# Expert weights asked for in the order in which pairs free their slots, and unread products moved, in a two-layer decoder step

## What is computed

```python
def _hier_moe(x, w_coarse, b_coarse, w_fine, b_fine, w_gate_up, w_down):
    ...
    for g in range(N_GROUPS):
        gate_g = jnp.where((grp == g)[:, None], gates, 0.0).astype(x.dtype)
        hg, hu = jnp.split(jnp.einsum('nd,edf->nef', xt, w_gate_up[g]), 2, axis=-1)
        out = out + jnp.einsum('nef,efd->nd', jax.nn.silu(hg) * hu * gate_g[..., None], w_down[g])
```

## Time and profile before

| what | value |
|---|---|
| runs | 1246.79, 1242.51 and 1245.45 us; median 1245.45 |
| profiled execution | 1240.65 us, span 1238.7 us, 15277 instructions |
| TensorE | busy 1115.0 us (90% of the span), mean granted clock 0.955 |
| VectorE, ScalarE, GpSimd | 504.6, 225.7 and 180.6 us |
| HBM | 342.75 MB read, 31.16 MB written; 302 GB/s over the span |
| asks for expert weights | 96 + 32 for gate and up, 56 + 8 for down, 1024 KB each |

### The profile page before, as it was taken

One profiled execution on the slowest core, in us unless ns is written; L12 is line 12 of the kernel. 1 busy time (PEld: TensorE's weight loads), 2 busy tenths in 40 slices (PEclk: granted clock), 3 DMA queues, 4 the chain that ended last, 5 costly groups with the idle time before them and its releaser, 6 DMA issues. The chain is left out here.

```text
span 1238.7 us, 15277 instructions
## 1 busy us (share of the span) xinstructions
PE 1115.0 (90%) x5797; PEld 565.1 (46%) x5797; DVE 504.6 (41%) x1368; ACT 225.7 (18%) x507; POOL 180.6 (15%) x177
## 2 busy tenths in 40 slices
PE   8999999999999978877899899999899999887872
PEld 6874666655543323323444346544554433332230
DVE  3614666567642211112432314553888322111117
ACT  1311233311121100001411213243212111000000
POOL 0000000000011111100634643220000111110203
PEclk9999899999999999889999999989899999998895
DMA  7520110439479999997967988884976899999955
GB/s 286 198 90 1 73 69 1 145 125 421 179 249 420 420 421 420 421 420 292 394 241 256 400 331 351 320 319 158 357 325 238 304 415 418 420 421 421 423 209 216
DMA packets 84955, 358.84 MB, mean 290 GB/s; under 512 B 13943, under 2 KB 18172, under 8 KB 55180
## 3 DMA queue, kind: packets, MB, share of 16 engines
q1 hardware_dynamic: 63276, 279.57, 56.8%
q0 software_dynamic: 19520, 74.01, 15.5%
q10 hardware_dynamic: 2080, 4.19, 0.9%
HBM read 342.75 MB, written 31.16 MB: 302 GB/s over the span
## 5 line engine op out<-in xcount | busy, mean ns | idle before, releaser
L1854 PE MATMUL ahead_psum<-m_wg,top_xT 128*64 128x512 f32 x704 | 202.1, 635 | 35.0 <-DMA m_wg<-in_moe_w_gate_up 28.2
L1854 PEld LDWEIGHTS ahead_psum<-m_wg,top_xT 128*64 128x64 f32 x704 | 61.2, 146 | 147.5 <-issue 102.7
L1879 PE MATMUL n_psum_m<-m_wd,top_xT 128*64 128x512 f32 x456 | 121.8, 604 | 1.6 <-ACT top_xT L1938 1.0
L1854 PE MATMUL ahead_psum<-top_wide,top_xT 128*64 128x512 f32 x288 | 100.0, 625 | 12.5 <-DMA top_wide<-in_moe_w_gate_up 6.4
L1333 PE MATMUL ahead_psum<-top_wide,top_xT 128*128 128x512 f32 x224 | 102.6, 603 | 1.5 <-PEq L159 1.5
L1920 DVE COPY top_xT<-n_psum_t 128x512 f32<-128x512 f32 x31 | 21.4, 691 | 185.3 <-PE n_psum_t L1839 185.3
L2307 PE MATMUL ahead_psum<-top_wide,top_xT 128*128 128x512 f32 x192 | 85.3, 595 | 4.3 <-DVE top_xT L2913 4.3
L1771 POOL DMA_INDIRECT expert_rows<-e_Y,m_dest x33 | 32.8, 994 | 380.2 <-DVE e_Y L1929 339.5
L2111 POOL DMA_INDIRECT cd_kv<-in_cache_kT,top_kpages x64 | 62.0, 969 | 65.4 <-PE cd_psum_d L2350 43.8
L1879 PEld LDWEIGHTS n_psum_m<-m_wd,top_xT 128*64 128x64 f32 x456 | 35.5, 138 | 56.5 <-issue 53.7
L1333 PEld LDWEIGHTS ahead_psum<-top_wide,top_xT 128*128 128x128 f32 x224 | 41.0, 192 | 44.2 <-issue 44.0
(11 more groups left out here) (517 smaller groups left out, 1706.3 us busy)
## 6 DMA issues: line engine op xcount, KB each, us to landing
m_wg<-in_moe_w_gate_up SPq DMA_DIRECT2D x96, 1024.0 KB, 26.7
m_wd<-in_moe_w_down SPq DMA_DIRECT2D x56, 1024.0 KB, 27.3
top_wide<-in_moe_w_gate_up SPq DMA_DIRECT2D x32, 1024.0 KB, 24.2
cd_kv<-in_cache_kT SPq DMA_DIRECT2D x64, 256.0 KB, 5.6
top_X<-in_moe_w_down SPq DMA_DIRECT2D x8, 1024.0 KB, 23.0
ab_w<-in_ab_w_in SPq DMA_DIRECT2D x2, 2048.0 KB, 11.5
top_wide<-in_ab_w_in SPq DMA_DIRECT2D x2, 2048.0 KB, 7.8
top_wide<-in_ab_w_out SPq DMA_DIRECT2D x2, 2048.0 KB, 8.6
```

Of the source, the lines that this page charges most:

```text
L1854: last = nc.tensor.matmul(pg[i % 2][64 * a:64 * a + 64, :], xgT[i % 2][:, j, 64 * a:64 * a + 64], wg[E.slot(i, a)][:, j * 512:(j + 1) * 51 ...
L1879: last = nc.tensor.matmul(py[n2][64 * a:64 * a + 64, :], hT[:, j, 64 * a:64 * a + 64], wd[E.slot(i, a)][:, j * D + n2 * 512:j * D + (n2 + ...
```

## The change

The loads are the same, and each waits for the same semaphore counts as before. What changes is the order: for each pair p, SyncE waits for gh and asks for the h0 of both experts whose slots p frees, then waits for gu and asks for both h1, then for dn and asks for both down weights. Ahead of the end it asks for the up halves of experts 29, 30 and 31 before the down weights of 29, 30 and 31. The 12 unread products behind the last regular pair are dropped in both layers, and the attention stage opens with 12 calls instead of 6.

```diff
--- before.py
+++ after.py
@@ -1177,9 +1177,9 @@
             return (2 * i + a) % self.RING
         return (((4, 0), (1, 2)), ((5, 6), (4, 0)))[self.l][(i - NE // 2) % 2][a]
 
-    def left(self, n):
-
-        return (n - self.RING) // 2 + 1
+    def after(self, p):
+
+        return [n for n in (2 * p + self.RING, 2 * p + self.RING + 1) if n < NE]
 
     def load_up(self, eng, n, halves=(0, 1)):
         for h in halves:
@@ -1192,17 +1192,18 @@
         row = (self.l * NE + n) * 128
         eng.dma_start(self.wd[n % self.RING][:, :], self.w_dn[row:row + 128, :]).then_inc(self.down_in[n // 2 % 4], 16)
 
-    def reload_up(self, eng, n, half_used, multiplied):
-
-        eng.wait_ge(half_used, self.left(n))
-        self.load_up(eng, n, (0,))
-        eng.wait_ge(multiplied, self.left(n))
-        self.load_up(eng, n, (1,))
-
-    def reload_down(self, eng, n, projected):
-
-        eng.wait_ge(projected, self.left(n))
-        self.load_down(eng, n)
+    def reload_up(self, eng, p, half_used, multiplied):
+
+        for h, used in enumerate((half_used, multiplied)):
+            eng.wait_ge(used, p + 1)
+            for n in self.after(p):
+                self.load_up(eng, n, (h,))
+
+    def reload_down(self, eng, p, projected):
+
+        eng.wait_ge(projected, p + 1)
+        for n in self.after(p):
+            self.load_down(eng, n)
 
     def fill(self, eng):
         for i in range(2):
@@ -1806,17 +1807,14 @@
         pool.sem_inc(all_landed, 1)
 
     def sync(sp):
-        E.reload_up(sp, 7, gh, gu)
-        E.reload_down(sp, 7, dn)
-        for n in range(8, NE - 4, 2):
-            E.reload_up(sp, n, gh, gu)
-            E.reload_up(sp, n + 1, gh, gu)
-            E.reload_down(sp, n, dn)
-            E.reload_down(sp, n + 1, dn)
-        for n in range(NE - 4, NE):
-            E.reload_up(sp, n, gh, gu)
-        for n in range(NE - 4, NE):
-            E.reload_down(sp, n, dn)
+        last = (NE - 1 - E.RING) // 2
+        for p in range(last - 1):
+            E.reload_up(sp, p, gh, gu)
+            E.reload_down(sp, p, dn)
+        E.reload_up(sp, last - 1, gh, gu)
+        E.reload_up(sp, last, gh, gu)
+        E.reload_down(sp, last - 1, dn)
+        E.reload_down(sp, last, dn)
         if lines:
             sp.dma_start(X[0:1, 4, :], lines[0].partition_broadcast(1)).then_inc(line_in, 16)
             sp.dma_start(xT[0:1, 4:8, 256:512], lines[1].rearrange("(o k n) -> o k n", o=1, k=4)).then_inc(line_in, 16)
@@ -1906,7 +1904,6 @@
         x_T(2)
         gate_up(1, 1)
         run(2, main)
-        idle_products(nc, C, unread, 12)
         tiles = tiles_of(pe)
         for (lo, hi), least in zip(parts, (0, 2)):
             with pe.If(tiles > least):
@@ -2472,7 +2469,7 @@
                     p_values(i - 2)
 
             front, back = range(KD // 2), range(KD // 2, KD)
-            idle_products(nc, C, bc, 6)
+            idle_products(nc, C, bc, 12)
             normal(0)
             idle_products(nc, C, bc, 4)
             project("q", "part")
```

## The result

The changed kernel takes **1229.38 us** (median of four executions, 1227.55 to 1231.06) beside 1244.62 us (four, 1242.51 to 1246.79) for the kernel before: ratio 0.9878, 95% interval 0.9838 to 0.9918. That is 15.2 us faster. I had forecast 1234.9 us, range 1230 to 1242: the direction is right, and the time lies 0.6 us under the range. The profiled execution after took 1231.06 us (span 1229.2), 9.6 us less than that of before (1240.65, span 1238.7); the sum of my steps was 10.6 us.

What follows compares the result with a forecast made beforehand. Weight loads, not products, were taken to set the pace of the expert stages. The terms -2.4 - 0.8 - 3.0 - 4.4 sum to -10.6 us, taken from 1245.45 us: 1234.9 us, range 1230 to 1242.

Steps and rivals of the forecast that it cites:

- the last one of the sum: Whole kernel: the profiled execution's 4.8 us under the median of three runs is carried over, so 1245.45 - 10.6 us.
- Order and lead: Expert stages: new order of asks with two blocks' lead starts the last gate 2.4 us earlier in layer 0, 3.0 in layer 1.
- the hole: Start of the expert reloads: DMA engines partly idle, 6.4 us unused in layer 0, 7.0 us in layer 1.
- The products dropped: Behind the last regular pair: nothing gained in layer 0; layer 1 behind the gate 4.4 us faster, bounds -5.3 and -0.6.
- the register read: Layer 1's extra pair: reading the tile count, perhaps covered by the dropped products, becomes exposed, +0.9 us.
- the weights: Layer 1, gate_up(16, 0): its second weights land at 1181.5, in time by 1.7 us for a start at 1183.2.
- The head: Attention stage's start: twelve calls hide an instruction fetch, transposes come 0.8 us earlier; ends -0.8 and +2.7, at worst +5.3.
- The rival (the stall stays where it is, +2.7): Attention stage's head: stall tied to entering the stage, head costs +2.7 instead of -0.8, 1238.4 us; chance 0.25.
- The warm gate: gate_up(14, 0), both layers: short TensorE idleness gives 3.55 us at full clock, 4.5 us more gained, 1230.3 us; chance 0.06.
- The dry stream: Expert stages: queue runs short of asks, each pair loses 2.6 us, 39 us in all, some 1279 us; chance 0.03.
- the order without the lead: Expert stages: other traffic takes the idle DMA time, gate 2.5 us later per layer, 1245.3 us, no change; chance 0.08.

Runs made afterwards that it cites:

- null: The kernel before, run once more unchanged: median 1245.88 us (12 executions), ratio 0.9982 to the kernel before.
- after_again: The changed kernel run again unchanged, beside other executions of the kernel before: 1234.25 us, ratio 0.9913.
- after_third: The changed kernel run once more unchanged, beside other executions of the kernel before: 1232.57 us (12 executions), ratio 0.9942.
- unread13: The kernel before with 13 unread products behind the last pair in place of 12: 1248.77 us, one execution.
- order_only: The kernel before with only the new order of asks, 12 unread products and 6 head calls kept: 1238.28 us (12 executions), ratio 0.9936.
- before_late_gather: The kernel before, with GpSimd gathering the extra pair's weights only once the last down blocks have landed: 1248.18 us (12 executions), ratio 1.0019.
- before_fill: The kernel before plus two calls of unread products in both layers' settle stage, ahead of the last row tile's second transposes: 1243.48 us (12 executions), ratio 0.9988.
- no_lead: The changed kernel, but expert 8's halves wait behind expert 7's down weights as before; new order from pair 1: 1243.75 us (12 executions), ratio 0.9982.
- tail_order: The changed kernel with another order of the last 15 asks, the four down blocks last: 1237.28 us (11 executions), ratio 0.9908.
- drop_only: The kernel before with only the 12 unread products behind the last pair dropped: 1241.46 us (12 executions), ratio 0.9957.
- drop_order_head6: The changed kernel with 6 calls of unread products at the attention stage's head in place of 12: 1234.17 us (12 executions), ratio 0.9942.
- head_only: The kernel before with only the attention stage's head calls raised from 6 to 12: 1247.63 us (12 executions), ratio 1.0029.

## Why the prediction missed, step by step

**The step that failed is the last one of the sum**: "The profiled execution took 1240.65 us ..., which is 4.8 us under the median of the three runs; I carry the difference over". That treats the distance of one execution to a median as a constant of the kernel. It isn't. The profiled execution of the changed kernel lay 1.7 us *over* its median, and those of null, after_again and after_third lie 1.7, 1.8 and 0.7 us over theirs. The miss is made up so: profiled difference 9.6 us where the sum had 10.6, +1.0; distance to the median 4.8 + 1.7, -6.5; together -5.5, which is 1229.4 less 1234.9. The range failed with it. Its low end was a mechanism (a warm clock at the gate) and left nothing for the executions themselves, though 1240.65 to 1246.79 stood in front of me.

Luck has a part on both sides. The medians of the changed kernel over 11 and 12 executions, 1234.25 and 1232.57 us, lie 0.7 and 2.3 us from the forecast and inside its range: the miss is as much that of a median of four as of the forecast. And that the two profiled executions differ by nearly what I summed is no proof of the steps. Followed through the two traces, the difference is 0.3 us ahead of layer 0's first gate, 3.5 in its experts, 1.4 to the transposes of the attention stage, then 3.4 us *lost* up to layer 1's first gate, 3.2 gained in its experts and 4.5 behind them. The part in between is not the change's: from those transposes to that gate single traces take 363.5 to 371.9 us, and on the mean 367.4 us with the old order and 367.5 us with the new (nine and seven traces). The trace of before had one of the shortest, 363.9 us.

**What makes executions differ** is in the traces, mostly far from the change: how long TensorE's clock stays at its lower level. Layer 0's mixer, TensorE's timeline of null, of before and of unread13 (16 matmuls of line 511, and in unread13 a second fall some 12 us later, seen in line 568's eight passes):

```profile
135.17 7.13 PE L511 MATMUL ab_psum<-top_wide,top_xT 128*128 128x512 f32 x16
```

```profile
136.20 9.71 PE L511 MATMUL ab_psum<-top_wide,top_xT 128*128 128x512 f32 x16
...
151.81 1.06 PE L568 MATMUL ab_psum<-top_consts,ab_later 128*128 128x128 f32 x8
```

```profile
136.20 10.07 PE L511 MATMUL ab_psum<-top_wide,top_xT 128*128 128x512 f32 x16
...
155.10 1.92 PE L568 MATMUL ab_psum<-top_consts,ab_later 128*128 128x128 f32 x8
```

The granted clock there (the column ahead of the DMA share), null, before, then unread13 with both of its falls:

```profile
135.00:140.00 5.00, 5.00 (x18) 2.20 (x13) 2.25 (x4) 0.00 (x0) 0.00 (x0) 1.00 0.38 157
```

```profile
135.00:140.00 5.00, 5.00 (x17) 2.60 (x16) 2.52 (x5) 0.00 (x0) 0.00 (x0) 0.50 0.34 143
```

```profile
135.00:140.00 5.00, 5.00 (x21) 2.60 (x18) 2.87 (x5) 0.00 (x0) 0.00 (x0) 0.53 0.28 116
...
150.00:155.00 5.00, 5.00 (x23) 4.26 (x20) 3.24 (x8) 0.42 (x1) 0.00 (x0) 0.50 0.56 210
```

The code and the data are the same up to here. The first pair's gate of layer 0 starts at 343.60, 346.68 and 352.50 us. Over all 18 traces its start follows the clock: where TensorE ran at the lower level for 3.4 us up to it (1.7 us lost) it comes at 343.4 to 344.4 us, where for 20.5 us (10.2 us lost) at 352.3 to 352.6 us. The same is seen in the settle stage of layer 1, in two executions of the changed kernel (its own trace, then that of after_again), 20 passes that pick rows:

```profile
939.93 5.54 PE L1391 MATMUL ahead_psum<-top_X,m_xg 32*128 32x512 f32 x8
...
945.96 5.42 PE L1391 MATMUL ahead_psum<-top_X,m_xg 128*128 128x512 f32 x12
```

```profile
940.06 7.49 PE L1391 MATMUL ahead_psum<-top_X,m_xg 32*128 32x512 f32 x8
...
948.38 7.44 PE L1391 MATMUL ahead_psum<-top_X,m_xg 128*128 128x512 f32 x12
```

The mean granted clock of these passes is 0.85 and 0.61. From the last row tile's transposes to the gate that is 16.4 us against 21.3 us. Over 18 traces this stretch takes 15.8 to 21.3 us in either layer, and layer 0's gate starts between 343.4 and 352.6 us. With the 7.8 us wait of null these are some 9 + 5 + 5 + 8 us that may or may not come, which covers the 19 us seen. The executions without a trace say the same: of the 20 of the kernel before that count beside after_third the five quickest took 1235.7 us on the mean at a granted clock of 0.9576, the five slowest 1245.5 us at 0.9538. As (1 - clock) x time that is 5 of the 10 us between them, so the clock is a large part and not all. The profiled execution of before had none of the long forms in either settle stage and no wait at down(15); that fits its low time, though one trace can't show that it is why.

**The terms of the sum**, over the traces with and without each (us; a single trace varies by 2 to 3):

| step | forecast | measured | from |
|---|---|---|---|
| layer 0, first gate to end of down(15) | -2.4 | -2.8 | 228.4 (9 traces of the old order) to 225.6 (7 of the new) |
| layer 1, the same | -3.0 | -3.1 | 228.5 (9) to 225.3 (7); -2.2 without null's 235.8 |
| head: down(15) to the transposes | -0.8 | about +0.4 | 16.0 (before 16.3, null and order_only 15.8, before_late_gather 16.0) to 16.4 (7, 14.9 to 17.8); before_fill, without the stall and with its six calls at a granted clock of 1.00, 12.9, where the transposes wait for ScalarE |
| layer 1, down(15) to the final products | -4.4 | -4.5 | 26.5 (before, null, order_only, before_fill) to 22.0 (9, 21.3 to 23.5) |

*Order and lead* were right in mechanism and in their sum: no_lead takes the gain away with the hole back. The two terms of the sum were each too large, by the gate in no_lead: 1.1 and 1.6 us for the order where I had 2.5, 3.5 and 3.4 us for the lead where I had 5.0 and more. Layer 0's last gate was forecast for 544.0 and came at 543.0, layer 1's for 1150.1 and came at 1149.1; counted from each layer's first gate, where the new execution was 0.3 and 1.8 us ahead, that is 0.7 us early and 0.8 us late.

*The products dropped*: right in size. The 0.9 us that I gave for the register read was nothing, and the weights, which I had 1.7 us early, came late: gate_up(16, 0) starts 2.76 us behind down(15), and 2.07 us where it doesn't wait for them (after_third, tail_order), so they cost 0.7 us here and up to 2.2 us in another trace (after_again, 4.30 us). The two nearly cancel (1181.1 measured at gate_up(16, 0), 1183.2 forecast, in an execution that was about 1 us further ahead at the gate).

*The head*: the stall went, as forecast, in all nine traces without the products. But the term was wrong in two ways. I called the dropped products of layer 0 free and let the entry follow down(15) by 7.6 us. Without them it comes 7.5 to 9.8 us after down(15), in five of nine traces 9.3 or more. In all nine SyncE's asks for the expert rows end 0.8 us ahead of it, so what is late is not TensorE: the scatter that they wait for takes 2.9 us to land in before and 5.3 us in after_again. Why it lands later when TensorE's unread products are gone, no run here shows. And the twelve calls cost their own time: drop_only and drop_order_head6, with six, reach the transposes after 14.8 us, no_lead, after_again and after_third, with twelve and as late an entry, after 16.7 to 17.8 us. The rival (the stall stays where it is, +2.7) is what head_only does, 18.7 us for 16.0 on the mean; in the changed kernel it fell.

*The warm gate*, the rival whose time was the nearest (1230.3), is not what happened: gate_up(14, 0) of the changed kernel runs at mixed clock (5.01 us as a whole in layer 0, 5.35 us in layer 1; 5.35 and 6.29 before), where 3.55 us would be the full clock; 0.3 and 0.9 us of the gain in these two traces lie in it. *The dry stream* and *the order without the lead* fell with the windows.

## What to carry to other kernels

A sum made on one trace forecasts the difference between traces; before it is put onto a median, read from several executions how far one lies from the next, and let the range hold that spread as well as the mechanisms. In a stage bound by loads, look where the transfer engines are idle at its start: two asks sent out there gave 3.5 us at the last gate of each layer, and the order alone, without them, gave nothing in the expert stages. Where a stage starts late, look which engine reached the barrier last before a cause is named: here it was SyncE in 17 of 18 traces, while my sum went by TensorE.

## What the runs showed of the hardware

- A stall of 3.4 us behind a jump, with an instruction packet inside it, that was gone with one unread product more or less (four instructions). With one more, all engines entered the stage 5.0 us behind SyncE's last ask in place of 0.8 us; with one fewer they did not.
- The same instructions on the same data ran at the lower clock for different stretches in different executions: 7.1, 9.7 and 10.1 us for one group of 16 matmuls, 11.0 and 14.9 us for 20 passes, at granted clocks of 0.85 and 0.61.
- In the expert stages asks of one queue landed in the order of asking. The last block of layer 1 landed after 35.9 us in null and some 39 us in tail_order, with another queue's four blocks asked for from 18.7 and 18.6 us behind it, and after 28.0 to 29.4 us in eight other traces; in layer 0, where no such asks follow, tail_order's took 28.4 us. In after_again they followed by 18.6 us too and nothing waited.
